# Other start addresses in SBUF for the operands of TensorE, in a hybrid diffusion step on one core

## The reference

```python
mc = jnp.split(silu(c_ctx)[None] @ w_ada + b_ada, 6, axis=-1)      # shift, scale, gate, twice; the same for c
h  = rms_norm(x, norm_mix) * (1 + scale1) + shift1
z, xbc, dt_f, dt_b, q, k, v, pin, gate_logits = split(h @ w_in)    # 2048 x 11296
y_ssd  = ssd_mixer(z, xbc, dt_f, dt_b, ...)        # bidirectional scan, conv of 5
o_attn = gqa_attend(q, k_all, v_all)               # 16 heads, 4 kv heads
o_pool = multiscale_pool(pin, pool_w, pool_scale)
merged = g0 * (y_ssd @ w_ssd_out) + g1 * (o_attn @ w_attn_out) + g2 * (o_pool @ w_pool_out)
x += gate1 * (merged @ w_out)
# MoE: 16 experts in 4 groups, top 2 inside the best group
a = einsum('bld,edf->blef', h2, w_gate);  u = einsum('bld,edf->blef', h2, w_up)
x += gate2 * einsum('blef,efd->bld', silu(a) * u * gate[..., None], w_down)
y = rms_norm(x, norm_final)
```

## Time and profile before

| | |
|---|---|
| median of three runs | 2038.82 us |
| the profiled execution | 2039.76 us |
| its span, first to last instruction | 2037.9 us |
| mean granted TensorE clock | 0.985 |
| TensorE busy | 1968.0 us (97%) |
| VectorE busy | 1483.3 us (73%) |
| ScalarE busy | 984.2 us (48%) |

### The profile page before, as it was taken

One profiled execution on the slowest core, in us unless ns is written; L12 is line 12 of the kernel. 1 busy time (PEld: TensorE's weight loads), 2 busy tenths in 40 slices (PEclk: granted clock), 3 DMA queues, 4 the chain that ended last, 5 costly groups with the idle time before them and its releaser, 6 DMA issues. The chain is left out here.

```text
span 2037.9 us, 27480 instructions
## 1 busy us (share of the span) xinstructions
PE 1968.0 (97%) x10588; PEld 1720.2 (84%) x10588; DVE 1483.3 (73%) x2130; ACT 984.2 (48%) x1468; POOL 7.1 (0%) x11
## 2 busy tenths in 40 slices
PE   7799999999999999999999999999999999999996
PEld 2299988997888999999999999996888888888884
DVE  0467676537988778785588884335799997999996
ACT  1233466332354332222333333333878887888883
POOL 0000000000000000000000000000000000000000
PEclk9999999999999999999999999997999999999998
DMA  9943333343433455555355557436799998999992
GB/s 376 399 145 135 125 130 119 109 145 123 150 132 142 166 187 206 206 207 196 109 206 207 207 188 262 165 122 239 281 379 370 358 357 284 365 354 365 361 360 109
DMA packets 133512, 460.94 MB, mean 226 GB/s; under 512 B 17568, under 2 KB 23520, under 8 KB 133248
## 3 DMA queue, kind: packets, MB, share of 16 engines
q1 hardware_dynamic: 133376, 459.12, 62.7%
HBM read 455.06 MB, written 4.00 MB: 225 GB/s over the span
## 5 line engine op out<-in xcount | busy, mean ns | idle before, releaser
L187 ACT ACTIVATE whi<-raw 128x1024 fp32r<-128x1024 f32 x640 | 678.7, 1061 | 778.2 <-PE bank L218 615.2
L193 DVE TENSOR_TENSOR wlo<-raw,whi 128x1024 fp32r<-128x1024 f32 x640 | 778.0, 1224 | 366.8 <-ACT whi L187 337.5
L213 PE MATMUL bank<-hhi,whi 128*128 128x384 f32 x1408 | 485.1, 345 | 8.9 <-PEq L1091 4.1
L214 PE MATMUL bank<-hlo,whi 128*128 128x384 f32 x1408 | 475.2, 338 | 0.0
L213 PEld LDWEIGHTS bank<-hhi,whi 128*128 128x128 f32 x1408 | 267.3, 190 | 26.1 <-issue 21.0
L218 PE MATMUL bank<-hhi,wlo 128*128 128x384 f32 x1408 | 273.7, 335 | 0.0
L214 PEld LDWEIGHTS bank<-hlo,whi 128*128 128x128 f32 x1408 | 267.9, 190 | 0.8
L276 DVE SCALAR_TENSOR_TENSOR cond_parts<-raw,cond_padded,cond_parts 128x512 f32<-128x512 f32 x360 | 250.6, 746 | 0.8 <-DVE rstd L71 0.2
L218 PEld LDWEIGHTS bank<-hhi,wlo 128*128 128x128 f32 x1408 | 248.2, 189 | 0.0
L2265 PE MATMUL bank<-whi,pair_tokens 128*128 128x512 f32 x512 | 201.7, 394 | 0.7 <-issue 0.7
L2266 PE MATMUL bank<-whi,pair_tokens 128*128 128x512 f32 x512 | 200.8, 392 | 0.0
(11 more groups left out here) (340 smaller groups left out, 2223.0 us busy)
## 6 DMA issues: line engine op xcount, KB each, us to landing
raw<-in_dense SPq DMA_DIRECT2D x448, 512.0 KB, 4.5
raw<-in_moe SPq DMA_DIRECT2D x384, 512.0 KB, 5.3
cs_rows_bc<-cs_rows SPq DMA_DIRECT2D x8, 768.0 KB, 5.1
merged<-in_x SPq DMA_DIRECT2D x4, 768.0 KB, 10.9
x_again<-in_x SPq DMA_DIRECT2D x4, 768.0 KB, 6.6
out_y<-y_normed SPq DMA_DIRECT2D x3, 768.0 KB, 4.5
shift_rows<-cs_rows SPq DMA_DIRECT2D x2, 1024.0 KB, 8.8
pool_w_sb<-in_pool_w SPq DMA_DIRECT2D x1, 1024.0 KB, 7.0
```

The source lines that it names most:

```text
L187: self.nc.scalar.activation(self.whi[:, k % W, :], self.raw[:, n % R, :], ACT.Copy).then_inc(self.hi_done, 1)
L193: self.nc.vector.tensor_tensor(self.wlo[:, k % W, :], self.raw[:, n % R, :], self.whi[:, k % W, :].bitcast(F32), ALU.subtract).then_inc(se ...
L213: self.nc.tensor.matmul(out, self.whi[:, s, c], xhi[:, k, :], start=(k == 0), stop=False)
L214: self.nc.tensor.matmul(out, self.whi[:, s, c], xlo[:, k, :], start=False, stop=False)
```

## The change

The two programs issue the same instructions in the same order on each engine. Only start addresses differ. The first free byte is rounded up by less, the small tensors are laid in another order, `hhi` starts at a multiple of 1024, `mods` (768 bytes) stands between `hhi` and `hlo`, `gains` (256 bytes) between `hlo` and `merged`, 64 bytes are left free ahead of `whi` and 32 ahead of `wlo`, and `a_exp` leaves the arena.

```diff
+LINE = 1024
@@ Net.__init__
-        self.at = (nc.sbuf_base + 63) // 32 * 32
+        self.at = (nc.sbuf_base + 31) // 32 * 32
         self.ident = sb("ident", [P, P], F32)
         self.ones = sb("ones", [P, P], F32)
-        self.mods = sb("mods", [P, 96, 2], F32)
-        self.gains = sb("gains", [P, 4, KB], F32)
         self.mod_a = sb("mod_a", [P, KB, 2], F32)
-        self.part_sums = sb("part_sums", [P, 2, KB], F32)
         self.rstd = sb("rstd", [P, T], F32)
         self.rs_v = sb("rs_v", [P, T], F32)
         self.rs_t = sb("rs_t", [P, T], F32)
+        self.part_sums = sb("part_sums", [P, 2, KB], F32)
+        self.a_exp = sb("a_exp", [P, 32], F32)
+        self.round_up()
         self.hhi_at = self.at
         self.hhi = sb("hhi", [P, KB, T], F32R)
+        self.mods = sb("mods", [P, 96, 2], F32)
         self.hlo_at = self.at
         self.hlo = sb("hlo", [P, KB, T], F32R)
+        self.gains = sb("gains", [P, 4, KB], F32)
         self.merged_at = self.at
         self.merged = sb("merged", [P, KB, T], F32)
         self.raw = sb("raw", [P, R, TILE], F32)
+        self.at += 64
         self.whi = sb("whi", [P, W, TILE], F32R)
+        self.at += 32
         self.wlo = sb("wlo", [P, W, TILE], F32R)
+    def round_up(self):
+        self.at = (self.at + LINE - 1) // LINE * LINE
@@ Scan
-        self.aexp = keep("a_exp", [P, 32], F32)
+        self.aexp = N.a_exp
```

## The result

The changed kernel is slower, by 0.4%: median 2046.23 us of twelve runs (2042.45 to 2051.51) against 2038.96 us of twelve (2033.23 to 2043.10), ratio 1.0037, 95% interval 1.0025 to 1.0049. That is +7.3 us (interval +5 to +10) where -22 were forecast. The time lies inside the stated range, 1968 to 2048, but on the other side of the kernel before.

A forecast was written before the change was run, and what follows sets the result against it. TensorE, by how close together its matmuls start, was taken as the bound. The terms 2.4 - 17.9 + 0 - 6.1 + 0 = -21.6 us led from the median 2038.8 to 2017 us, range 1968 to 2048.

The forecast's parts named there:

- (e): `raw` written at a new start address, Scalar- and VectorE reading at other addresses: counted 0, bounds 2 us to either side.
- (b): Line 214 on `hlo`, 218 on `hhi`, `ssd_out`/`pool_out` with `whi` at untried distances: -5 ns for 3584 matmuls, -17.9 us.
- (d): Experts, lines 2265 and 2266 from distance -64 to -32: -4 ns for 1536 matmuls, -6.1 us; line 2270 stays.
- (a): Line 213 on `hhi` goes to distance +64: 1.7 ns more for each of 1408 matmuls, +2.4 us.
- (c): `merged`, line 213 at distance +32 and line 214 at +64: counted 0, bounds 0.5 us to either side.
- Rival 2: Dense matmuls: distance 0 is quiet, any other breaks the rhythm; +8.5 us at 1.7 ns, +25 at 5; chance 0.16.
- Rival 1: All matmuls: distance all but irrelevant, each weight line read costs a fixed time; 2039, within 0.3%; chance 0.33.
- Rival 3: Dense and expert matmuls: far enough apart, streams never collide; 1934, smaller form 1987; chance 0.10 for both.
- the 13.3 ns: Dense matmuls at full clock: part of 173.3 ns beyond the 160 for 384 columns; 82 us over 6144 matmuls.

## Why the prediction was wrong

The reading of what bounds the kernel held: TensorE sets the end, and what its streams lost or won went through to the time. The sum over the kinds gives the difference of the medians within 0.7 us for the changed kernel and two of the other repeated ones; for the one without fillers it is 3.5 us off, unexplained. The transfers and the splitting of tiles did not move, as (e) had it. What failed is the sign of (b) and (d).

**(a)** Near in its number, +2.4 us forecast for line 213 and +1.9 in the trace, but partly by luck. In the run at +64 alone line 213 rose by 0.2 ns, +0.3 us, and not by 1.7. On line 213 at +64, line 214 at the equivalent +64 and line 218 at +96, the runs with one distance have +0.3, +0.9 and +1.3 us, +2.4 together; the changed kernel, which mixes them, lost 5.0. That mixing costs by itself is what this suggests; no run tests it alone.

**(b)** Wrong, and the step that decided. -5 ns for 3584 matmuls, -17.9 us, rested on "the new distances are up to three times as long" and on the shortest duration seen, 331 ns. The trace has +4.1 us on them: line 214 +1.1, line 218 +2.0, `ssd_out` and `pool_out` with `whi` +1.0 (the last need not come from their own distance: in the run at +32 they rose by 0.9 us at an unchanged 0). Two errors are in it. A longer distance is not a longer one: -192 is +64, and 128 is as far as it goes, and the worst. And 331 was never a short matmul by itself: a short distance between starts is one beat of a rhythm whose others are long. One such rhythm in the changed kernel is 174, 178, 171, 177 ns, mean 175. A minimum taken from durations that vary is no estimate of what a steady stream would have; the row of `hlo` at distance 0 in the earlier trace rows has the same minimum, 331, so that it did not set the distances apart at all. And the 384 on `wlo` at distance 0, which I let stand, lost 0.5 us; that they follow tiles that are out of step is the likely reason, not a tested one.

**(c)** -0.4 us, within its bounds.

**(d)** Wrong in the same way: -6.1 us from the minimum 387 beside the median 392. The trace has +1.3 us on the lines at -32 and -0.4 on the one that stayed, together no more than the 0.8 to 1.0 us by which the experts drifted in other runs at unchanged distances. What is shown is that nothing was won, and that distance 0 wins 3.9 to 4.4 us there.

**Rival 2** (0 is a quiet distance, and any other breaks the rhythm) is nearest to what came, at 0.16 of the chances: it named +8.5 us at 1.7 ns a matmul, and +7.3 were measured. The number fits better than the mechanism: +32 and -64 turned out as quiet on lines 213, 214 and 218. Its place was only partly right. The 4224 matmuls on `hhi` and `hlo` rose by 5.0 us, 1.2 ns each, less than the 1.4 from which I said it decides; the other 2.3 us came from `ssd_out` and `pool_out` (+1.5), the experts (+0.9), `pick` and `w_dt` (+0.4), less `merged` (-0.4). (Its middle, 2053, is misreckoned: half way between +8.5 and +25 is 2055.6. And the 4.07 us that the forecast named for a tile is 4.09 by its own terms. Neither changes the argument.)

**Rival 1** is wrong: the effect of distance is real and repeats at +256 to 0.03 ns. The rule of the Trainium skill, page "SBUF — State Buffer", section "Who interferes with whom", that the two read ports of TensorE are independent, does not agree with the traces if it is read, as the prediction read it, to mean that addresses cannot matter: the same instructions differ by up to 2.5 ns with nothing moved but their operands (173.6 at 0, 176.1 at +128 on line 214).

**Rival 3** and its time are gone for the distances tried: with 0 seven of the eight multiples of 32 below 256, and none has a line of `hhi` or `hlo` below 173.2 ns on the mean.

Not settled: why the streams lock at some distances, what makes a stream fall into the slow pace, and what the 13.3 ns are. That they come from the two streams meeting was argued from the half clock, where they vanish; the run with half the weight columns speaks against a price in proportion to the columns loaded. Distances that are no multiple of 32, and +160, were not tried.

## What to carry to other kernels

When a long stream of equal matmuls is the bound, read the distance between starts for each pair of operands over the whole trace, and ask whether it is one number or a rhythm: a minimum of a rhythm is not to be had alone, only its mean. Keep the two operands at one distance that is known to lock (0 did here for 384 and 512 columns; modulo 256, as far as tried) instead of spreading them, and count each kind by its columns, since `pick` with 256 columns wanted what the others did not. And compare profiles of single executions only after the granted clock: the difference between 0.985 and 0.982 was worth some 5 us here, beside 7.3 for the whole change.

## What the runs showed of the hardware that was not expected

- The distance between the start addresses of the moving and the stationary float32r operand changes how close matmuls start, modulo 256 bytes in the two pairs tried: 173.6 ns at 0 and +256, 174.2 at +64 and +320, 176.1 at +128 (means of line 214).
- At one and the same distance, +64, a stream keeps either of two paces over many tiles: 4.16 us or 4.24 us for 24 matmuls of 384 columns. The distance changes how often the slow one comes.
- In step, a float32r matmul takes 32 cycles of 2.4 GHz more than its columns at the lengths that occur here: 173.3 ns for 384 and 226.7 for 512; with all at distance 0 those of 256 columns have 119.8 to 120.5 on the mean, where 288 cycles are 120.0. With 64 weight columns in place of 128 one of 384 columns takes no less (174.9 ns).
- At +64 the 256-column matmuls with `pick` take 115.7 to 117.2 ns, less than those 32 cycles allow: distance 0 is not the best for every length.
- At the lower clock, 1.2 GHz, 384 columns take 0.32 us and nothing is left over the earlier trace rows; the same 0.32 us stand in the traces of the changed kernel and of the run at +128.
